# Third memory-key unit in front of the first layer norm, one fewer among the attention pairs, and earlier rounding of queries' and keys' parts

## The reference, cut to what matters

```python
q, k, v = jnp.split(h @ w_in, 3, axis=-1)          # stick-breaking attention, 16 heads
o = stick_breaking_core(_heads(q, 16), _heads(k, 16), _heads(v, 16))
h = layer_norm(ALPHA * h + merge(o) @ mix_wo, g0, b0)
q = _heads(h @ xa_wq, 4)                            # attention to 256 memory rows
k, v = jnp.split(mem @ xa_wkv, 2, axis=-1)
p = jax.nn.softmax(jnp.einsum('bhtd,bhmd->bhtm', q, k) * 256 ** -0.5, axis=-1)
h = layer_norm(ALPHA * h + merge(p @ v) @ xa_wo, g1, b1)
```

## Time and profile before

| what | us |
|---|---|
| median of three runs | 1365.0 |
| the profiled execution, its own time | 1364.36 |
| its span, first to last instruction | 1362.6 |
| PE busy (99% of the span) | 1344.8 |
| POOL busy | 811.6 |
| DVE busy | 834.7 |
| ACT busy | 702.3 |

### The profile page before, as it was taken

How to read it: one execution, slowest core, us unless ns; L and a number is a source line. 1 busy time by engine, 2 the same in 40 slices (tenths; PEclk the granted TensorE clock), 3 DMA queues, 4 the chain that set the end, 5 groups by cost and what they waited for, 6 DMA issues and landing times.

```text
span 1362.6 us, 24461 instructions
## 1 busy us (share of the span) xinstructions
PE 1344.8 (99%) x9730; PEld 1148.5 (84%) x9730; DVE 834.7 (61%) x1073; ACT 702.3 (52%) x1236; POOL 811.6 (60%) x601
## 2 busy tenths in 40 slices
PE   9999999999999999999999999999999999999998
PEld 7888787778899898988888887788888878999987
DVE  5135465466556887885545967344279857777732
ACT  4245566463457566665322478466473525445543
POOL 6643332563366876766655647854268856666782
PEclk9999999999999999999999999999999999999999
DMA  6332221221240223233333212200023222333322
GB/s 228 124 124 77 78 78 47 94 92 62 76 142 32 93 93 109 91 111 105 111 108 109 94 63 93 78 4 4 19 77 124 94 92 94 109 96 106 102 99 77
DMA packets 34517, 122.94 MB, mean 90 GB/s; under 512 B 3824, under 2 KB 4336, under 8 KB 34288
## 3 DMA queue, kind: packets, MB, share of 16 engines
q1 hardware_dynamic: 33696, 119.31, 26.1%
q10 hardware_dynamic: 720, 2.20, 0.5%
HBM read 119.40 MB, written 2.10 MB: 89 GB/s over the span
## 4 chain that ended last, share of the span: by engine, by line
PE 86%; DVE 4%; POOL 3%; issue 3%; ACT 2%; DMA 1%; SPq 0%; ACTq 0%; POOLq 0%; DVEq 0%
PE ps L624 13%; PE ps L626 13%; PE ps L625 13%; PE ps L1515 3%; PE ps L1517 3%; PE ps L1516 3%; POOL w_lo L2390 2%; PE ps L1026 2%; PE ps L1027 2%; PE ps L1028 2%; PE ps L1584 1%; PE ps L1583 1%; PE ps L1585 1%; PE ps L764 1%; PE ps L980 1%
## 5 line engine op out<-in xcount | busy, mean ns | idle before, releaser
L2390 POOL TENSOR_TENSOR w_lo<-stage,w_hi 128x512 fp32r<-128x512 f32 x346 | 511.7, 1503 | 328.0 <-ACT w_hi L1614 321.7
L1614 ACT ACTIVATE w_hi<-stage 128x512 fp32r<-128x512 f32 x312 | 178.9, 623 | 114.1 <-DMA stage<-w 99.0
L624 PE MATMUL ps<-x_hi,w_lo 128*128 128x512 f32 x536 | 213.1, 398 | 0.0
L625 PE MATMUL ps<-x_lo,w_hi 128*128 128x512 f32 x536 | 208.9, 390 | 0.0
L626 PE MATMUL ps<-x_hi,w_hi 128*128 128x512 f32 x536 | 208.8, 390 | 0.0
L624 PEld LDWEIGHTS ps<-x_hi,w_lo 128*128 128x128 f32 x536 | 100.7, 188 | 23.9 <-issue 2.6
L626 PEld LDWEIGHTS ps<-x_hi,w_hi 128*128 128x128 f32 x536 | 100.6, 188 | 21.4
L625 PEld LDWEIGHTS ps<-x_lo,w_hi 128*128 128x128 f32 x536 | 100.7, 188 | 20.8 <-issue 1.0
L2593 POOL TENSOR_TENSOR w_lo<-stage,w_hi 128x512 fp32r<-128x512 f32 x44 | 75.4, 1742 | 54.1 <-DVE s_val L3388 54.1
L2446 POOL TENSOR_TENSOR w_lo<-stage,w_hi 128x512 fp32r<-128x512 f32 x32 | 55.3, 1757 | 34.3 <-DVE us_val L2993 34.3
L2697 DVE TENSOR_TENSOR_SCAN ps<-ps,self_one 128x512 f32<-128x512 f32 (+1 forms) x64 | 49.2, 814 | 26.2 <-ACT ps L1676 26.2
(11 more groups left out here) (558 smaller groups left out, 3839.0 us busy)
## 6 DMA issues: line engine op xcount, KB each, us to landing
stage<-w SPq DMA_DIRECT2D x210, 512.0 KB, 3.5
extra_stage<-w SPq DMA_DIRECT2D x6, 512.0 KB, 5.5
H<-xT SPq DMA_DIRECT2D x3, 512.0 KB, 8.6
mem<-memT SPq DMA_DIRECT2D x2, 512.0 KB, 10.6
pool_n<-pool_count ACTq DMA_DIRECT2D x1, 1024.0 KB, 5.7
outT<-outs SPq DMA_DIRECT2D x4, 256.0 KB, 2.0
outT<-outs SPq DMA_DIRECT2D x2, 384.0 KB, 2.7
stage<-w SPq DMA_DIRECT2D x2, 256.0 KB, 4.1
```

Source lines behind the costliest of these rows:

```text
L624: pe.matmul(out, wl, hi(k), start=first, stop=False)
L625: pe.matmul(out, wh, lo(k), start=False, stop=False)
L1614: act.activation(unit_hi(b)[:, cols], unit_stage(b)[:, cols], ACT.Copy).then_inc(whi_made, 1)
L2390: pool.tensor_tensor(unit_lo(b)[:, cols], unit_stage(b)[:, cols], unit_hi(b)[:, cols].bitcast(F32), ALU.subtract).then_inc(wlo_made, 1)
```

## The change

It has five parts.

1. `MK_PAIRS` goes from 6 to 5. The sixth pair (g = 5) loses its memory-key unit and takes the order of a pair without one. The stage `sb` has 37 units in place of 38, the stage `mem` three in place of two, and the third uses bank 7. `FIRST_TURNED` is not changed.
2. The rounding of units is renumbered with it. The first query unit is now rounded behind the norm's root, where the second was, and the second between the norm's tiles: on ACT behind tile 1's `H`, on POOL behind `x_lo(1)`.
3. `two_products` gets another order of slots for the query units: three of the first unit, three of the second, then in turn.
4. `mk_hi` lies at another address (24 in place of A0 + 81, where the memory's own high part lies), so that head 0's `mk_hi` and `mk_lo` no longer wait for the last memory keys to be taken.
5. The factor 1/16 goes from the softmax into the taking of the queries; the maximum is taken negated, and the multiplication at line 2803 goes.

```diff
-STAGE_UNITS = [("sb", 38), ("wo", 8), ("mem", 2), ...
+STAGE_UNITS = [("sb", 37), ("wo", 8), ("mem", 3), ...
+XA_SCALE = float(D // XA_HEADS) ** -0.5
-PAIR_UNIT = [18, 21, 24, 27, 30, 33, 36, 38]
-MK_PAIRS = 6
+PAIR_UNIT = [18, 21, 24, 27, 30, 33, 35, 37]
+MK_PAIRS = 5
-        mk_hi = at("mk_hi", [P, KB, MEM], A0 + 81, F32R)
+        mk_hi = at("mk_hi", [P, KB, MEM], 24, F32R)
@@ PE
             mem_product(U0["mem"], 4, between={4: wo_sums})
             mem_product(U0["mem"] + 1, 5)
+            mem_product(U0["mem"] + 2, 7)
@@ PE, two_products of the query units
-                             lambda k: (x_ready, k + 1 + BEFORE["x_ready"]["wo"]))
+                                 lambda k: (x_ready, k + 1 + BEFORE["x_ready"]["wo"]),
+                                 [(n, k) for n in range(2) for k in range(3)] + [(n, k) for k in range(3, KB) for n in range(2)])
@@ ACT, pair
-                split_hi(PAIR_UNIT[0] + 2 + 3 * g if not last else U0["wo"] + 2)
+                ahead = PAIR_UNIT[0] + 2 + 2 * g + min(g, MK_PAIRS)
+                split_hi(ahead)
@@ ACT, statistics and scale_shift
-                    split_hi(U0["xq"] + 1 if n == "wo" else U0[n] + UNITS_OF[n] - 1 + AHEAD)
+                    split_hi(U0["xq"] if n == "wo" else U0[n] + UNITS_OF[n] - 1 + AHEAD)
-                with act.Fori(0, KB) as k:
+                for k in range(KB):
...
+                    if k == 1:
+                        split_hi(U0["xq"] + 1)
@@ ACT, xa_soft and the taking of the queries
-                                   bias=soft_max[:, h, t:t + 1], scale=float(D // XA_HEADS) ** -0.5,
+                                   bias=soft_max[:, h, t:t + 1],
-                    take(xq_hi[:, 2 * h + d, :], u % 2, u + CREDIT + 1)
+                    take(xq_hi[:, 2 * h + d, :], u % 2, u + CREDIT + 1, scale=XA_SCALE)
@@ POOL, split_x
-                with pool.Fori(0, KB) as k:
+                for k in range(KB):
...
+                    if k == 1:
+                        split_lo(U0["xq"] + 1)
@@ DVE, xa_soft
-                                      ALU.max).then_inc(xa_max, 1)
-                dve.wait_ge(xa_max, 3 * h + 2)
-                dve.tensor_scalar(soft_max[:, h, :], soft_max[:, h, :], -float(D // XA_HEADS) ** -0.5, None,
-                                  ALU.mult).then_inc(xa_max, 1)
+                                      ALU.max, negate=True).then_inc(xa_max, 1)
@@ DVE, xa_parts
-                if h == 0:
-                    dve.wait_ge(evac, EV0["xq"] + CREDIT)
+                if h in (0, XA_HEADS - 1):
+                    dve.wait_ge(evac, EV0["xq" if h else "mem"] + CREDIT)
-                    dve.tensor_tensor(xq_lo[:, 2 * h + d, :], ps[:, d, :], xq_hi[:, 2 * h + d, :].bitcast(F32),
-                                      ALU.subtract).then_inc(xa_split, 1)
+                    dve.scalar_tensor_tensor(out=xq_lo[:, 2 * h + d, :], in0=ps[:, d, :], scalar=XA_SCALE,
+                                             in1=xq_hi[:, 2 * h + d, :].bitcast(F32), op0=ALU.mult, op1=ALU.subtract).then_inc(xa_split, 1)
```

More of the change, by code:

```diff
@@ L36 @@
 SCRATCH = 1024
-STAGE_UNITS = [("sb", 38), ("wo", 8), ("mem", 2), ("xq", 8), ("xo", 8), ("up", 44), ("down", 24),
+STAGE_UNITS = [("sb", 37), ("wo", 8), ("mem", 3), ("xq", 8), ("xo", 8), ("up", 44), ("down", 24),
                ("rwkv", 17), ("conv", 16), ("pool", 8), ("branch", 36), ("out", 8)]
@@ L61 @@
 FIRST_Q, FIRST_K = 12, 17
-PAIR_UNIT = [18, 21, 24, 27, 30, 33, 36, 38]
-MK_PAIRS = 6
+PAIR_UNIT = [18, 21, 24, 27, 30, 33, 35, 37]
+MK_PAIRS = 5
 Q_UNITS = [FIRST_Q] + PAIR_UNIT[:PAIRS - 1]
 K_UNITS = [FIRST_K] + [PAIR_UNIT[g] + (2 if g < MK_PAIRS else 1) for g in range(PAIRS - 1)]
-MK_UNITS = [PAIR_UNIT[g] + 1 for g in range(MK_PAIRS)] + [U0["mem"], U0["mem"] + 1]
+MK_UNITS = [PAIR_UNIT[g] + 1 for g in range(MK_PAIRS)] + [U0["mem"] + n for n in range(KB - MK_PAIRS)]
 Q_TAKEN = [1] + [3 * g for g in range(1, PAIRS)]
-K_TAKEN = [2] + [3 * g + 2 if g <= MK_PAIRS else 3 * g + 1 for g in range(1, PAIRS)]
+K_TAKEN = [2 * g + 2 + min(g, MK_PAIRS) for g in range(PAIRS)]
 MK_TAKEN = [3 * g + 4 for g in range(MK_PAIRS)]
@@ L375, in build_block @@
         n_ev = 0
-        for name, n in (("sb", 22), ("wo", 0), ("mem", 2), ("xq", 8), ("xo", 0), ("up", 44), ("down", 0),
+        for name, n in (("sb", 21), ("wo", 0), ("mem", 3), ("xq", 8), ("xo", 0), ("up", 44), ("down", 0),
                         ("rwkv", 17), ("conv", 16), ("pool", 8), ("branch", 24), ("out", 9)):
@@ L1682, in pair @@
                 turned_taken(g, 0)
-                split_hi(PAIR_UNIT[0] + 3 + 3 * g if not last else U0["wo"] + AHEAD)
+                split_hi(ahead + 1)
                 turned_taken(g, 1)
@@ L1688, in pair @@
                 if g < MK_PAIRS:
-                    split_hi(PAIR_UNIT[0] + 4 + 3 * g)
+                    split_hi(ahead + 2)
                 take_k(g + 1)
@@ L1726, in statistics @@
                 if both:
-                    split_hi(U0["xq"] + 1 if n == "wo" else U0[n] + UNITS_OF[n] - 1 + AHEAD)
+                    split_hi(U0["xq"] if n == "wo" else U0[n] + UNITS_OF[n] - 1 + AHEAD)
             def scale_shift(n):
-                v = KB * NORMS[n]
-                with act.Fori(0, KB) as k:
+                for k in range(KB):
                     act.wait_ge(normed, k + 1 + BEFORE["normed"][n])
-                    shift = V("ln_b", v + k)
+                    shift = V("ln_b", KB * NORMS[n] + k)
                     act.activation(x_hi[:, k, :], Y[:, k, :], ACT.Identity, bias=shift).then_inc(xhi_made, 1)
                     act.activation(H[:, k, :], Y[:, k, :], ACT.Identity, bias=shift).then_inc(h_made, 1)
+                    if k == 1:
+                        split_hi(U0["xq"] + 1)
             tiles("wo")
@@ L1741, in _ @@
             for n in range(UNITS_OF["mem"]):
-                take_mem(U0["mem"] + n, 4 + n)
+                take_mem(U0["mem"] + n, (4, 5, 7)[n])
             split_hi(U0["xq"] + 2)
             def xa_soft(h):
-                act.wait_ge(xa_max, 3 * h + 3)
+                act.wait_ge(xa_max, 2 * h + 2)
                 if h >= 2:
```

## The result

The changed kernel takes **1370.81 us** (median of 7 runs, 1368.06 to 1371.46) beside 1365.0 us for the kernel before (7 runs, 1364.22 to 1365.64): a ratio of 1.0037, interval 1.0027 to 1.0046. It is 5.8 us slower where I had forecast 2.1, and 2.5 us above the upper end of my range. Its profiled execution has an own time of 1371.32 us and a span of 1369.6, 7.0 more than the span before.

What follows compares the result with a forecast made beforehand. PE was taken as the bound, with an unchanged matmul count, so only its waiting could change. 1.53 + 0.35 + 0.45 - 0.20 = +2.13 us on 1365.0 gave 1367.1 us, range 1365.0 to 1368.3.

Steps and rivals of the forecast that it cites:

- part 1: Sixth pair: 1.34 us shorter, not 2.87, so everything up to the norm comes 1.34 us earlier.
- three places that matter: The two kinds of pair, the query units, and the hand-over to the scores with head 3's softmax wait.
- The times that I gave as signs: Profile: memory units end near 285.9, mk_hi starts 290.5, last five query matmuls near 298.4, scores 300.9.
- only waiting can come or go: PE: no matmul added or dropped, so only time in which PE stands waiting can change.
- Sixth pair, +1.53: Pair lasts 19.30 us, 1.34 shorter, while the third memory unit adds 2.87 before the query units: +1.53 us.
- Query units, +0.35: After six matmuls PE waits for POOL's second-unit w_lo; arrival to end of issue 13.67 us against 13.32: +0.35.
- Order of the slots, +0.45: Before the scores: first query unit ends two matmuls nearer the end; the 0.86 us behind issue becomes 1.31: +0.45.
- Keys, 0: Head 0's earlier mk_hi and mk_lo move nothing; beside them POOL's x_lo loses 1.28 us, still in time.
- The fourth rival: DVE holds up POOL's x_lo, six at 1.74 us each: +3.4 us in all, 1368.4 us; chance 0.13.
- Head 3, -0.20: Head 3's softmax: without the multiplication PE's 0.36 us wait for the weights shrinks by 0.20 us.
- Slower by over 0.2%: Whole kernel over 1367.7 us, from POOL held up by DVE and the forecast's upper end; chance 0.19.
- All rivals: Neither wait, 0.05; only sixth pair waits, 0.10; only POOL late, 0.10; POOL held up by DVE, 0.13.

Runs made afterwards that it cites:

- experiment 1: Changed kernel with the Q_TAKEN table corrected, so the seventh pair's q_lo waits for taking 20, not 21: 1367.68 us beside 1364.81, ratio 1.0021.
- experiment 2: Kernel before with the wrong Q_TAKEN count alone, the last q_lo waiting for the taking of the last keys: 1367.44 us beside 1364.81, ratio 1.0021.
- experiment 6: On experiment 1, eight unread 512-column matmuls put in front of PE's wait for w_lo: 1366.64 us beside 1365.08, ratio 1.0009.
- experiment 3: On experiment 1, the sixth pair's second head also copied in two parts (added to FIRST_TURNED): 1367.09 us beside 1364.81, ratio 1.0017.
- experiment 9: Kernel before with the new order of query-unit slots alone: 1365.39 us in one execution, beside 1365.0.
- experiment 7: On experiment 4, head 0's keys made while DVE waits for the means, PE waiting for each unit half apart: 1364.89 us beside 1365.08, ratio 0.9995.
- experiment 4: On experiment 3, second query unit rounded earlier, its remainders before all x_lo, old order of slots: 1364.90 us beside 1364.81, ratio 1.0000.
- experiment 8: On experiment 7, the last tile's x_lo made by DVE in place of POOL: 1363.85 us (12 runs) beside 1365.08, ratio 0.9994.

## Why the prediction was wrong

- **The step that failed** is the sentence in part 1 that "everything up to the norm comes 1.34 us earlier". I had named three places that matter and took all between them, the seventh pair among them, to be only shifted: a term of nothing without a reason. The seventh pair took 3.59 us more, 1.92 of waiting for `q_lo` and 1.70 at half the clock less 0.03, and the eighth began 2.80 us later (228.71 for 225.91). The times that I gave as signs were late with it: 290.32 for 285.9 at the end of the memory units, 294.79 for 290.5 at `mk_hi`, 302.89 for 298.4 at the last five matmuls, 305.14 for 300.9 at the scores. The cause of the wait was visible before the run. Removing one taking from the sixth pair renumbers all takings behind it, and one waiter held its number in a table of its own. I had priced only what the diff showed to move. That cost 1.92 us (experiments 1 and 2).
- **The clock was left out.** I wrote that only waiting can come or go. A wait of about 2 us, of which my own forecast contained one, was followed in part of the executions by some 3.4 us at half the clock, which cost 1.70 us in `pv` and 1.56 behind `w_lo` (experiment 1). On the median this is about 1.3 us behind `w_lo` alone (experiment 6), and the changed kernel has two such places. With the count right the kernel is 2.9 us above the one before (experiment 1), where I had 2.1.
- **Sixth pair, +1.53:** right in place and size (19.30 us, 1.48 idle on `soft`, 2.73 from the transposes to `pv`), and the single copy was its reason (experiment 3).
- **Query units, +0.35:** right. PE did six matmuls, waited 0.20 for `x_hi` and 2.02 for `w_lo`. From the last memory matmul to the end of issue it took 302.89 + 5 x 0.227 - 290.32 = 13.70 us; forecast 13.67.
- **Order of the slots, +0.45:** the mechanism right, the size too large. It measured 0.25 in the changed kernel (305.14 - 304.02 = 1.12 against 0.86) and 0.38 alone (experiment 9), one trace each. ACT's two takings took 1.09 and not 1.28.
- **Keys, 0:** right, and `x_lo` lost 8.20 - 6 x 1.26 = 0.64 us to them, half of the 1.28 that I had allowed. I had taken the 0.64 of the earlier trace rows for one instruction, but both ran into those three halves (`mk_hi` until 296.53, the halves from 296.21). Nor did they cost POOL their whole length, as I reasoned there: alone they take 0.42 and 0.69 us (experiment 7), 1.11 together. The fourth rival had the right side but the wrong reason: POOL was in time for all tiles. The loss began to count only when the wait in front of it had been shortened (experiment 4).
- **Head 3, -0.20:** right (0.16 left of 0.36).

The sum of the parts: 2.13 - 0.20 (the slots) + 1.92 + 1.70 for one fall = 5.55, beside the measured 5.8. That these agree so well is in part luck: how many falls the median run had is not known (it reads 0.999), and the profiled one, with one fall, has 1.4 us in places that the sum leaves out. The two lowest runs, at a clock of 1.000, lie at 1368.06 and 1368.85, beside 1365.0 + 2.13 - 0.20 + 1.92 = 1368.85.

The chances were off as well. Slower by over 0.2% had 0.19, most of it on POOL being held up by DVE, which is not what happened. All rivals were about the places of the diff; none asked what else reads the numbers that the change shifts.

## What to carry to other kernels

When a change adds or drops an event that a semaphore counts, list every waiter on that semaphore, also in lines that the diff leaves alone. A count that is too high breaks nothing and only costs time, so nothing but the profile shows it. In a trace such a wait can be known by its releaser: an instruction whose result the waiting one does not read.

Where TensorE is the bound, price a stop of about 2 us at more than its length, as the falls behind such waits teach. Unread matmuls in an unavoidable gap can pay for themselves, as they did here by about 1.3 us. Whether several short waits are cheaper than one of the same sum was not tested by itself; no trace shows a fall behind a short one. And before a mean clock is read as a sign, see what it reads in traces that have no fall.

## What the runs showed of the hardware

- TensorE's granted clock fell to 0.50 at waits of 2.0 to 2.1 us, in part of the executions of one and the same kernel. The traces have eight such waits and three falls, of 3.41 us each; two began 0.34 and 0.74 us behind the wait's end, the third 0.15 us ahead of it (experiment 3). Where the cost could be read it was 1.70 and 1.56 us. No fall stands in the traces at the waits of 1.48, 0.92 and 0.79 us.
- Such waits are not the only cause. One run of experiment 8 is at 0.997 and 1369.38 us, and two of the 79 runs of the kernel before beside the experiments are at 0.998 (1366.66 and 1368.13), though no wait in the traces of these two kernels is longer than 1.5 us. What disturbed them is not known.
- The half clock ended within an unbroken row of matmuls: in experiment 1 their distance is 0.43 us until 293.86 and 0.23 from 294.24 on, with no wait between.
- A conversion and a subtraction of 128x512 on DVE beside POOL's subtractions cost POOL 0.64 and 0.65 us together, in two kernels. They were themselves slower there: 1.05 and 1.67 us, where the same two take 0.42 and 0.69 with POOL idle (experiment 7).
